# Feed-forward inner groups turned in 32x32 blocks by VectorE and carried by SBUF transfers, in place of TensorE transposes

## The reference, cut to what matters

```python
def swiglu_ffn(h, w_gate_up, w_down):      # h: 256 x 1024, w_gate_up: 1024 x 5632, w_down: 2816 x 1024
    gate, up = jnp.split(h @ w_gate_up, 2, axis=-1)
    return (jax.nn.silu(gate) * up) @ w_down
```

## Time and profile before

| | |
|---|---|
| median of the runs | 1648.66 us |
| span of the profiled execution, first to last instruction | 1646.2 us |
| TensorE busy | 1626.7 us (99%) |
| VectorE busy | 973.8 us (59%) |
| ScalarE busy | 788.2 us (48%) |
| TensorE clock granted, mean | 0.997 |
| HBM traffic | 175 GB/s, DMA engines about half busy |

### The profile page before, as it was taken

How to read it: one execution, slowest core, us unless ns; L and a number is a source line. 1 busy time by engine, 2 the same in 40 slices (tenths; PEclk the granted TensorE clock), 3 DMA queues, 4 the chain that set the end, 5 groups by cost and what they waited for, 6 DMA issues and landing times.

```text
span 1646.2 us, 18705 instructions
## 1 busy us (share of the span) xinstructions
PE 1626.7 (99%) x7962; PEld 1334.2 (81%) x7962; DVE 973.8 (59%) x1008; ACT 788.2 (48%) x961; POOL 70.7 (4%) x100
## 2 busy tenths in 40 slices
PE   9999999999999999999999999999999999999999
PEld 7877877888888888798888888977788887678887
DVE  5655675655456544746644566778645447955453
ACT  5445444543444434455634355745544345844342
POOL 0000000100001000100100000010000002000000
PEclk9999998999999999999999999999999999999999
DMA  9544442454545545453545454443455445245451
GB/s 364 184 178 180 179 166 103 167 216 179 192 168 206 202 179 204 160 217 129 205 179 205 179 192 179 157 138 68 163 208 201 179 157 204 80 154 195 173 195 48
DMA packets 51967, 289.33 MB, mean 176 GB/s; under 512 B 14215, under 2 KB 14855, under 8 KB 19114
## 3 DMA queue, kind: packets, MB, share of 16 engines
q1 hardware_dynamic: 51596, 287.54, 48.2%
q10 hardware_dynamic: 288, 0.59, 0.1%
HBM read 287.06 MB, written 1.05 MB: 175 GB/s over the span
## 4 chain that ended last, share of the span: by engine, by line
PE 90%; DVE 6%; ACT 2%; issue 1%; POOL 1%; DMA 0%; SPq 0%; DVEq 0%; ACTq 0%
PE ps L538 86%; PE ps L642 2%; PE ps L547 1%; DVE wl L1972 1%; ACT wh L1289 1%; DMA raw<-in_w 0%; DVE tmp L2003 0%; DVE x L2005 0%; POOL st L2730 0%; DVE smg L2642 0%; POOL st L2727 0%; DVE xc L2465 0%; DVE scg L2655 0%; DVE smn L2468 0%; PE ps L1146 0%
## 5 line engine op out<-in xcount | busy, mean ns | idle before, releaser
L1972 DVE TENSOR_TENSOR wl<-raw,wh 128x2048 fp32r<-128x2048 f32 x256 | 579.6, 2287 | 151.6 <-ACT wh L1289 151.5
L538 PE MATMUL ps<-wh,xTh 128*128 128x512 f32 x1408 | 557.3, 396 | 2.6 <-DVE xTl L2449 0.7
L538 PE MATMUL ps<-wh,xTl 128*128 128x512 f32 x1408 | 549.8, 391 | 0.0
L538 PE MATMUL ps<-wl,xTh 128*128 128x512 f32 x1408 | 549.3, 390 | 0.0
L1289 ACT ACTIVATE wh<-raw 128x2048 fp32r<-128x2048 f32 x256 | 481.2, 1910 | 7.5 <-PE ps L538 4.4
L538 PEld LDWEIGHTS ps<-wh,xTh 128*128 128x128 f32 x1408 | 264.9, 188 | 66.7 <-issue 6.4
L538 PEld LDWEIGHTS ps<-wh,xTl 128*128 128x128 f32 x1408 | 264.9, 188 | 56.3
L538 PEld LDWEIGHTS ps<-wl,xTh 128*128 128x128 f32 x1408 | 265.1, 188 | 52.8
L2727 POOL TENSOR_SCALAR st<-st 128x1 f32<-128x1 f32 (+2 forms) x46 | 30.6, 664 | 1389.6 <-ACT tmp L1308 813.8
L1352 ACT ACTIVATE sgf<-ps,st 128x256 f32<-128x256 f32 x22 | 10.4, 475 | 103.1 <-PE ps L538 103.1
L1352 ACT ACTIVATE sge<-ps,st 128x256 f32<-128x256 f32 x22 | 10.4, 474 | 96.6 <-PE ps L538 96.6
(11 more groups left out here) (340 smaller groups left out, 2270.1 us busy)
## 6 DMA issues: line engine op xcount, KB each, us to landing
raw<-in_w SPq DMA_DIRECT2D x256, 1024.0 KB, 4.8
gains<-in_rows SPq DMA_DIRECT2D x18, 512.0 KB, 4.2
raw<-in_w SPq DMA_DIRECT2D x8, 512.0 KB, 9.6
nab<-in_rpb SPq DMA_DIRECT2D x32, 32.0 KB, 2.5
out_x<-x SPq DMA_DIRECT2D x2, 512.0 KB, 2.6
x<-in_x ACTq DMA_DIRECT2D x1, 512.0 KB, 6.0
x<-in_x SPq DMA_DIRECT2D x1, 512.0 KB, 9.7
nabfirst<-in_rpb SPq DMA_DIRECT2D x16, 32.0 KB, 2.7
```

Of the source, the lines that this page charges most:

```text
L538: return pe.matmul(o, lhs, rhs, start=start, stop=stop, skip_group_check=False)
L1972: TT(wl[:, p % RAW, :], raw[:, p % RAW, :], wh[:, p % RING, :].bitcast(F32), ALU.subtract).then_inc(*lo(p))
```

## The change

For groups 1 to 9 the transposes of line 642 are gone from TensorE. VectorE, right after each product, turns it in 32x32 blocks into `hs` (`block`). ScalarE then starts 16 transfers from SBUF to SBUF (`move`), one for each pair of a source band and a destination band of 32 partitions: block row a, column c goes to row c, place a of `hx`. For groups 1 to 8 a transfer has 32 rows of 512 bytes and carries both token halves. For group 9 the halves go apart (`parts`): 16 transfers for t = 0, begun between ScalarE's gate(9, 0) and gate(9, 1), and 16 for t = 1 after the two pieces of weights, each of 32 rows with two runs of 128 bytes. ScalarE and VectorE make `hTh` and `hTl` from `hx` at the head of the next iteration (`gather`). TensorE's dn(9, t) waits for its own half. ScalarE's silu waits for the product of two groups before instead of the transposes. Groups 0 and 10 stay as they were. (`by_dma` is not called.) In stage a's memory plan two inputs share their room with their low parts, which makes place for `hs` and `hx`.

```diff
+def parts(j):
+    return ((0,), (1,)) if j >= NJ - 2 else ((0, 1),)
 # tensor_program, ffn
-                    on.wait_ge(hT_lo, f, j, t if j == NJ - 1 else 0)
+                    on.wait_ge(hT_lo, f, j, t if j >= NJ - 2 else 0)
                 gate(1, 1, lambda: turn(0, (0, 1)))
                 dn(0, 0)
-                turn(1, (0, 1))
                 dn(0, 1)
                 for j in range(2, NJ - 1):
                     gate(j, 0)
                     gate(j, 1)
                     dn(j - 1, 0)
-                    turn(j, (0, 1))
                     dn(j - 1, 1)
 # scalar_program
+            def move(f, j, ts):
+                r = rooms[f]
+                on.wait_ge(blocked, f, j, ts[-1])
+                if j >= 3:
+                    on.wait_ge(hT_lo, f, j - 2, 0)
+                for a in range(4):
+                    for c in range(4):
+                        src, dst = r.hs[32 * a:32 * a + 32, j % 2, c, :, :, :], r.hx[32 * c:32 * c + 32, j % 2, a, :]
+                        if len(ts) == 1:
+                            src, dst = src[:, :, ts[0], :], dst.rearrange("p (k t n) -> p k t n", k=2, t=2)[:, :, ts[0], :]
+                        else:
+                            src = src.rearrange("p k t n -> p (k t n)")
+                        s = moved_in(f, j, ts[0])
+                        act.dma_start(dst, src).then_inc(*s[0](f, j, ts[0], a, c, by=16))
 ...
-                        on.wait_ge(turned, f, j - 2, 0)
+                        on.wait_ge(product, f, j - 2, t)
+                def gather(j):
+                    for ts in parts(j):
+                        on.wait_ge(*moved_in(f, j, ts[0]))
+                        if j >= 2:
+                            on.wait_ge(multiplied, ffn_rows(f, j - 2))
+                        dst, src = in_order(r, j, ts)
+                        act.activation(dst(r.hTh), src, ACT.Copy).then_inc(*hT_hi(f, j, ts[0]))
 ...
                     ring.need(p + 2)
+                    gather(j - 1)
                     gate(j, 0)
+                    if j == NJ - 2:
+                        move(f, j, (0,))
                     gate(j, 1)
                     ring.fill(2, p + 2)
+                    move(f, j, parts(j)[-1])
                     ring.need(p + 3)
-                    turn(j, (0, 1))
                     ring.fill(1, p + 3)
 # vector_program
+                def block(j, t):
+                    on.wait_ge(product, f, j, t)
+                    dve.transpose(r.hs[:, j % 2, :, :, t, :].rearrange("p c k n -> p k c n"), r.hb[:, j % 2, t, :].rearrange("p (k c n) -> p k c n", k=2, c=4)).then_inc(*blocked(f, j, t))
+
+                def gather(j):
+                    for ts in parts(j):
+                        on.wait_ge(hT_hi, f, j, ts[0])
+                        dst, src = in_order(r, j, ts)
+                        TT(dst(r.hTl), src, dst(r.hTh).bitcast(F32), ALU.subtract).then_inc(*hT_lo(f, j, ts[0]))
 ...
+                    gather(j - 1)
                     gate(j, 0)
+                    block(j, 0)
                     gate(j, 1)
+                    block(j, 1)
                     ring.fill(2, p + 2)
                     ring.need(p + 3)
-                    turn(j, (0, 1))
                     ring.fill(1, p + 3)
```

More of the change, by code:

```diff
@@ L208, in ffn_rows, with by_dma @@
     return FIRST[f] + (3 * j + 4 if j < NJ - 1 else 32)
+def by_dma(j):
+    return 0 < j < NJ - 1
+def parts(j):
+    return ((0,), (1,)) if j >= NJ - 2 else ((0, 1),)
 def pair_bank(j, t):
@@ L322, in ffn_room @@
             r.hb = sb(f"hb{f}", [128, 2, 2, 256], F32, ph)
+            r.hs = sb(f"hs{f}", [128, 2, 4, 2, 2, 32], F32, ph)
+            r.hx = sb(f"hx{f}", [128, 2, 4, 128], F32, ph)
             return r
@@ L337, in build @@
             cv.dfh = sb("dfh", [128, N_DFT], F32R, early)
+            with ExitStack() as same:
+                cv.df = sb("df", [128, N_DFT], F32, same)
             cv.dfl = sb("dfl", [128, N_DFT], F32R, early)
             with ExitStack() as ph:
-                cv.df = sb("df", [128, N_DFT], F32, ph)
                 cv.brow = sb("brow", [2, D], F32, ph)
-                cv.taps = sb("taps", [TAPS, D], F32, ph)
                 cv.th = sb("tapsh", [TAPS, D], F32R, ph)
+                with ExitStack() as same:
+                    cv.taps = sb("taps", [TAPS, D], F32, same)
                 cv.tl = sb("tapsl", [TAPS, D], F32R, ph)
@@ L440, in build @@
         nab_in = [steps(f"nab{i}") for i in range(4)]
+        blocked = steps("blocked")
+        moved = [steps(f"moved{n}") for n in range(2)]
         def split_of(p):
@@ L449, in lo_part, with moved_in, in_order @@
             return wl[:, p % RAW, :].rearrange("p (k n) -> p k n", k=k)
+        def moved_in(f, j, t):
+            return moved[t if j == NJ - 2 else j % 2], f, j, t, 3, 3
         def halves(b, n=4):
             return bank(b).rearrange("p (k n) -> p k n", k=n)
+        def in_order(r, j, ts):
+            if len(ts) == 2:
+                return (lambda h: h[:, j % 2, :, :, :].rearrange("p k t (a n) -> p a (k t) n", a=4),
+                        r.hx[:, j % 2, :, :].rearrange("p a (m n) -> p a m n", n=32))
+            return (lambda h: h[:, j % 2, :, ts[0], :].rearrange("p k (a n) -> p a k n", a=4),
+                    r.hx[:, j % 2, :, :].rearrange("p a (k t n) -> p a k t n", k=2, t=2)[:, :, :, ts[0], :])
         GROUPS = (2, 3, 0, 1)
@@ L1374, in ffn @@
                 ring.need(p0 + 5)
-                turn(1, (0, 1))
+                move(f, 1, (0, 1))
                 for j in range(2, NJ - 1):
@@ L2056, in ffn @@
                 gate(1, 0)
+                block(1, 0)
                 ring.fill(2, p0)
@@ L2061, in ffn @@
                 gate(1, 1)
+                block(1, 1)
                 ring.fill(5, p0 + 4)
                 ring.need(p0 + 5)
-                turn(1, (0, 1))
                 for j in range(2, NJ - 1):
```

## The result

The changed kernel takes 1799.27 us (median of four runs, 1796.33 to 1800.91) beside 1648.1 us for the kernel before: a ratio of 1.0918 (95% interval 1.0903 to 1.0933). It is 151 us slower. The forecast was 1700 us and its range ended at 1745. The sign and the place were right, the size was not.

A forecast was written before the change was run, and what follows sets the result against it. TensorE, busy 99%, was taken to bound the kernel. 1648.7 us, plus 43 for group 9's stands in six stages net of the removed transposes, plus 9 of clock, gave about 1700 us; range 1632 to 1745.

The forecast's parts named there:

- What bounds, and what goes: TensorE, busy 99%, bounds the kernel; dropping its transposes in 54 groups saves 0.44 us each, 23.8 us in all.
- the pace of an issue: ScalarE's transfer issues: 0.44 us each for groups 1 to 8 (7.0 us a group), 0.55 for group 9 (8.8 a half).
- rival 2: Group 9's half transfers cost 0.654 us an issue: stand of 14.6 us, net 10.7 a stage, 1728 us; chance 0.10.
- Hidden with 2.8 us to spare: Groups 1 to 8: turned data ready at T+13.6, TensorE's down products need them at T+16.37, so no wait.
- Group 9: At each stage's end its two rows of issues make TensorE stand 11.1 us, net 7.15 us lost, 43 in six stages.
- Issues beside A and B: ScalarE's issues start when the block is done, T+1.75, beside copies A and B rather than behind them.
- rival 1: Strict turns on ScalarE: issues begin only after copies A and B, at T+4.28; 1739 us, chance 0.20.
- Clock: TensorE's matmuls after its stands run at half clock, 1.5 us a stage, 9 us in all.
- DMA load, block transpose, SBUF sources: DMA engines go from 53% to 59% busy, a VectorE block takes 0.5 us, copies from SBUF keep PSUM times; no cost.

The follow-up runs named there:

- experiment 9: Kernel before plus rows of eight DMA issues of different forms ending ScalarE's and SyncE's programs; only issue lengths read: 0.61 us SBUF to SBUF, 0.44 from HBM.
- experiment 6: Changed kernel with stage a's small table operations right behind the blocks, beside the issues, instead of between piece C and the gather: 1786.5 us, ratio 1.0844.
- experiment 8: Changed kernel with unread matmuls, 34 and 29, in TensorE's two stands of each stage: 1790.91 us, ratio 1.0875.
- experiment 1: Changed kernel without any transfers, block transposes and gathers kept, off-diagonal blocks left in the wrong band: 1621.19 us, ratio 0.9838.

## Why the prediction was wrong, step by step

- **What bounds, and what goes: right.** Without the transfers the stages gain 26.5 us; 23.8 was worked out from the earlier trace rows.
- **The step that failed: the pace of an issue.** I took 0.44 us for whole rows and 0.55 us for halves, from ScalarE's two loads. Both forms take 0.645 us, so a row of 16 takes 10.3 us, not 7.0 and 8.8. The rows that I leaned on are loads from HBM; experiment 9 shows that the same form costs 0.61 us instead of 0.44 when both sides lie in SBUF. I treated 0.654 us as the price of a third dimension and gave rival 2, which has it for the halves, a chance of 0.10. Even that rival left the whole rows at 0.44 us.
- **"Hidden with 2.8 us to spare": fell with it.** The loop of an ordinary group is 1.75 + 10.3 + 1.9 + 2.3 + 0.7 = 17.0 us, over TensorE's 16.37. Seven groups wait 4.7 us together in stage b. In stage a the small tables stand in the same loop: its period is 18.7 us, and I had weighed them only against the spare 2.8. Stage a lost 21 us more than b; experiment 6 takes back 12.8 of them, and about 7 are the wait in its first group, whose issues stand behind late weights. The forecast had no term for that.
- **Group 9: mechanism right, price too low.** The two rows of 16 stand one behind the other ahead of C, as forecast, with a wait for wl before the one for hTl (3.4 and 7.7 us forecast, 8.1 and 6.7 measured). Counted as the forecast counts, TensorE begins dn(9, 0) in stage b at T+28.2 us (537.81 less 509.59) and wanted to at T+10.94: 17.3 us late instead of 11.1. It stands for 14.8 of them, and 2.4 are the twelve matmuls between the stands at the half clock. The forecast's own chain at 10.3 us a row gives 11.1 + 3.0, and 2.6 more because hTl of group 8 now comes late and the first row starts at T+0.85 instead of T-1.75: 16.7 us. That the standing alone is near rival 2's 14.6 us is chance, since rival 2 means the whole delay and has no late start.
- **Issues beside A and B: right.** So rival 1's order did not come about, though its 1739 us would have been the nearest of the numbers. By the Trainium skill (Perfetto Trace Analysis, DVE / Act Engine Instruction) the sequencer is free once it has pushed an instruction; the trace agrees (442.68 beside 441.09 and ahead of 442.89).
- **Clock: forecast 9 us, measured 8.4** by experiment 8 for the stages' ends, though 20 matmuls a stage run slow there: most of them inside a wait that ScalarE ends. The slow matmuls behind stage a's first stand come on top and were not forecast.
- **DMA load, block transpose, SBUF sources: right.** The moves take 3.4% of the engines' time, a block 0.45 us (0.5 taken), and experiment 1 shows the rest hidden.
- **The range was too narrow** because towards the slow side it took the unknown pace as unknown in one place only, the halves of group 9. With the measured pace a stage loses 16.7 us in group 9 and, as measured in b, 4.7 in the groups before it, less 3.95; six of these are 105 us. With stage a's measured 21 and 9 of clock the sum is 1648.7 + 105 + 21 + 9 = about 1784 us. Of the 16 us that are left, 8.7 are what stages c to f lost more than b; why they did was not followed.

## What to carry to other kernels

Count the issues of small transfers as work of the engine that issues them, at a price from a row with the same kind of source and destination; where no such row exists, carry the dearest bound through every step that uses it, since a loop that is just covered turns at a threshold. Put such a row of issues on the engine whose program has the room, and count how many rows fall in one period there: eight groups on SyncE gained 1.5%, the ninth in halves, gathered late, lost it again. A split that starts the consumer earlier is no help when it doubles a fixed price per part.

## What was not expected of the hardware

- From SBUF to SBUF an issue takes 0.61 us on ScalarE and 0.59 us on SyncE, from 1 row to 128 and from 512 bytes to 128 KB in all; with an HBM source 0.44 and 0.42 us, and 0.346 us for a store from SBUF to HBM on SyncE. In a stream single issues take up to 1.8 us.
- ScalarE's issues pass its queued copies, but they begin behind a copy's wait for weights: 6 us after the block was done in stage a's first group (43.03 and 36.78 us).
- ScalarE issues transfers beside its own queued instructions: two copies of 1.9 us stood in the queue, not begun, when the first issue passed them (148.84 us, experiment 6).
- VectorE turns 128x256 floats in 32x32 blocks in 0.45 us, about what the product of that size takes (0.48 us).
- Matmuls put into TensorE's stands held the granted clock at 1.00, but won back only what lay behind the last stand.
